# Routing the sample tokens through both row halves of TensorE in the first gather of a mixture-of-experts kernel

## What is computed

```python
h = rmsnorm(x, norm_ffn)                      # x * rsqrt(mean(x*x)) * gain
g_idx = argmax(h @ router_g + b_g)            # one of 4 groups
top_v, top_i = top_k(e_logits[g_idx], 2)      # two of the group's 4 experts
hid = silu(h @ w_gate[e]) * (h @ w_up[e])     # 256 wide
y = sum over the two experts of weight * (hid @ w_down[e])
x = x + y
```

## Time and profile before

| what | value |
|---|---|
| median of 3 runs | 586.61 us (585.15 to 587.17) |
| profiled execution, its own time | 584.05 us |
| its span, first to last instruction | 581.9 us |
| mean granted TensorE clock | 0.995 of full speed |
| PE busy | 558.2 us (96% of the span) |
| DVE, ACT, POOL busy | 247.4, 154.7, 79.4 us |
| moved by transfers | 208.94 MB, mean 359 GB/s |

### The profile page before, as it was taken

The page is one execution under the profiler, slowest core; times in us unless marked ns, Lnnn a source line. Parts: engine busy times, 40 slices in busy tenths (PEclk is TensorE's granted clock), DMA queues, the critical chain, the costliest instruction groups (busy, mean ns, idle before and its releaser), DMA issues. The chain is left out here.

```text
span 581.9 us, 8509 instructions
## 1 busy us (share of the span) xinstructions
PE 558.2 (96%) x3438; PEld 309.4 (53%) x3438; DVE 247.4 (43%) x559; ACT 154.7 (27%) x327; POOL 79.4 (14%) x116
## 2 busy tenths in 40 slices
PE   6999999999999999998999999999999889999993
PEld 5777877544633333337876556667644533333331
DVE  6999783223651112145633415260113642211146
ACT  6132195121301101134235104164003220101023
POOL 5960800000121110000100001000000011220000
PEclk9999999999999999999999999999999999999997
DMA  8995999997999999999999998999699999999872
GB/s 329 415 355 79 222 401 380 375 403 318 363 410 420 419 419 422 395 306 374 390 412 317 409 400 335 304 355 409 256 407 417 381 406 417 420 419 423 358 234 91
DMA packets 40073, 208.94 MB, mean 359 GB/s; under 512 B 12835, under 2 KB 14563, under 8 KB 24192
## 3 DMA queue, kind: packets, MB, share of 16 engines
q1 hardware_dynamic: 30560, 169.93, 74.9%
q0 software_dynamic: 7872, 34.53, 16.6%
q10 hardware_dynamic: 1600, 3.90, 1.7%
HBM read 198.77 MB, written 43.74 MB: 417 GB/s over the span
## 5 line engine op out<-in xcount | busy, mean ns | idle before, releaser
L1513 PE MATMUL bank<-arena 128*64 128x512 f32 x264 | 85.6, 598 | 0.5 <-DVE arena L1853 0.5
L1513 PE MATMUL bank<-ring,arena 128*64 128x512 f32 x232 | 74.7, 598 | 0.1
L2310 PE MATMUL bank<-arena,ring 128*128 128x320 f32 x256 | 71.6, 434 | 0.0
L2310 PEld LDWEIGHTS bank<-arena,ring 128*128 128x128 f32 x256 | 48.0, 190 | 21.4 <-issue 1.6
L1434 PE MATMUL bank<-ring,arena 128*128 128x512 f32 x92 | 40.3, 594 | 1.0 <-PEq L455 0.6
L1513 PEld LDWEIGHTS bank<-arena 128*64 128x64 f32 x264 | 24.0, 136 | 31.5 <-issue 31.3
L1544 PE MATMUL bank<-arena 128*64 128x512 f32 x136 | 39.8, 594 | 0.7 <-ACT arena L1758 0.7
L577 PE MATMUL bank<-xnT,ring 128*128 128x320 f32 x144 | 39.5, 434 | 0.5 <-DVE xnT L896 0.5
L1969 DVE COPY arena<-bank 128x512 f32<-128x512 f32 x14 | 9.7, 692 | 68.3 <-PE bank L1544 68.3
L1544 PE MATMUL bank<-ring,arena 128*64 128x512 f32 x120 | 36.1, 593 | 0.7 <-ACT arena L1758 0.7
L1513 PEld LDWEIGHTS bank<-ring,arena 128*64 128x64 f32 x232 | 20.8, 136 | 24.5 <-issue 24.3
(11 more groups left out here) (446 smaller groups left out, 846.5 us busy)
## 6 DMA issues: line engine op xcount, KB each, us to landing
arena<-in_w_moe SPq DMA_DIRECT2D x50, 1024.0 KB, 17.4
ring<-in_w_moe SPq DMA_DIRECT2D x44, 1024.0 KB, 17.2
arena<-in_stream_b SPq DMA_DIRECT2D x4, 2560.0 KB, 14.8
out_o_d_old<-in_cache_d_g POOLq DMA_DIRECT2D x1, 8448.0 KB, 30.4
arena<-in_stream_a SPq DMA_DIRECT2D x4, 2048.0 KB, 10.8
out_o_d_old<-in_cache_d_g POOLq DMA_DIRECT2D x1, 7680.0 KB, 41.9
out_o_d_old<-in_cache_d_g SPq DMA_DIRECT2D x1, 4608.0 KB, 37.8
ring<-in_w_out_even SPq DMA_DIRECT2D x2, 2048.0 KB, 11.3
```

The lines of the kernel that those rows point to most:

```text
L1513: last = nc.tensor.matmul(c.bank[2 + j % 2][half, :], xgT[:, j % 2, q, half], w[i][q // 4][:, q % 4, :], start=(q == 0), stop=(q == KC - 1))
L2310: last = nc.tensor.matmul(bank(name)[:, 0:TOK], w[:, k, i * P:(i + 1) * P], xnT[:, k, :], start=(k == 0), stop=(k == KC - 1))
```

## The change

It touches `moe_block` alone, in both layers. Tile 2's normed rows and one-hot matrix are laid out on all 128 partitions: partitions 0 to 63 hold columns 0 to 511 of the 64 sample rows, partitions 64 to 127 hold columns 512 to 1023 of the same rows, and `Sf[:, 2]` is there twice. `gather_samples` replaces `gather_first(2)`: the same 8 products, in the order (q, half), where half 0 runs on the rows 0 to 63 of the array into bank 2 and half 1 on the rows 64 to 127 into bank 3. `tmp` for the upper partitions is made by one more DVE instruction on the two columns that `Sf` needs. ACT writes the samples' normed rows with two activations in place of one, and their transfer to `x_rows` runs over 128 partitions with 2 KB each, where it was 64 with 4 KB each. The first copy out of bank 2 is split in two (q = 0, 1 and q = 2, 3), so that there are three `xt_ok` signals for pair 0, and `up(0)` writes bank 4 in place of bank 2.

```diff
@@ -1235,6 +1235,10 @@
     def gathered_rows(j):
 
         return m["xg"][(j - 1) % XG]
+
+    def up_bank(j):
+
+        return 2 + j % 2 if j else 4
 
     def yo_of(j):
 
@@ -1388,7 +1392,7 @@
 
         @block.gpsimd
         def _(pool):
-            nc.gpsimd.memset(xn[64:P, 2], 0.0).then_inc(gather_steps, 1)
+            nc.gpsimd.memset(xn[:, 2], 0.0).then_inc(gather_steps, 1)
 
             def gather(j):
 
@@ -1481,16 +1485,25 @@
             def gather_first(t, first=0, end=KC):
 
                 for q in range(first, end):
-                    last = nc.tensor.matmul(c.bank[2 + q // 4][:, (q % 4) * P:(q % 4 + 1) * P], xn[0:ROWS[t], t, q * P:(q + 1) * P],
-                                            m["Sf"][0:ROWS[t], t].rearrange("p e s -> p (e s)"),
-                                            start=(t == 0 and q % 4 == 0), stop=(t == 2 and q % 4 == 3))
-                    if t == 2 and q % 4 == 3 or t == 0 and q == KC - 1:
+                    last = nc.tensor.matmul(c.bank[2 + q // 4][:, (q % 4) * P:(q % 4 + 1) * P], xn[:, t, q * P:(q + 1) * P],
+                                            m["Sf"][:, t].rearrange("p e s -> p (e s)"), start=(t == 0 and q % 4 == 0), stop=False)
+                    if t == 0 and q == KC - 1:
                         last.then_inc(first_pe, 1)
 
+            def gather_samples():
+
+                for q in range(4):
+                    for h in range(2):
+                        half = slice(64 * h, 64 * h + 64)
+                        last = nc.tensor.matmul(c.bank[2 + h][:, q * P:(q + 1) * P], xn[half, 2, q * P:(q + 1) * P],
+                                                m["Sf"][half, 2].rearrange("p e s -> p (e s)"), start=False, stop=(q == 3))
+                        if q == 3:
+                            last.then_inc(first_pe, 1)
+
             def turn(j):
 
                 gathered(pe, j)
-                pe.wait_ge(xt_ok, 2 * j)
+                pe.wait_ge(xt_ok, 2 * j + 1)
                 for q in range(KC):
                     last = nc.tensor.transpose(c.bank[q // 4][:, (q % 4) * P:(q % 4 + 1) * P], gathered_rows(j)[:, q * P:(q + 1) * P],
                                                c.ident[:, :])
@@ -1502,15 +1515,17 @@
                 if first == 0:
                     piece_arrived(pe, 6 * j)
                     piece_arrived(pe, 6 * j + 1)
-                    pe.wait_ge(xt_ok, 2 * j + 1)
+                    pe.wait_ge(xt_ok, 2 * j + 2 if j else 1)
                 for q in range(first, end):
+                    if j == 0 and q == 2:
+                        pe.wait_ge(xt_ok, 2)
                     if q == KC // 2:
-                        pe.wait_ge(xt_ok, 2 * j + 2)
+                        pe.wait_ge(xt_ok, 2 * j + 3)
                         piece_arrived(pe, 6 * j + 2)
                         piece_arrived(pe, 6 * j + 3)
                     for i in range(2):
                         half = slice(64 * i, 64 * i + 64)
-                        last = nc.tensor.matmul(c.bank[2 + j % 2][half, :], xgT[:, j % 2, q, half], w[i][q // 4][:, q % 4, :],
+                        last = nc.tensor.matmul(c.bank[up_bank(j)][half, :], xgT[:, j % 2, q, half], w[i][q // 4][:, q % 4, :],
                                                 start=(q == 0), stop=(q == KC - 1))
                     if q == KC // 2 - 1:
                         last.then_inc(up_mid, 1)
@@ -1603,8 +1618,8 @@
                 last = nc.tensor.matmul(c.bank[7][:, 64:80], ones, m["sum"][:, u, :], start=(u == 0), stop=(u == 2))
             last.then_inc(pos_pe, 1)
             pe.wait_ge(S0_ok, 2)
-            pe.wait_ge(xn_ok, 3)
-            gather_first(2)
+            pe.wait_ge(xn_ok, 4)
+            gather_samples()
             up(0, 0, 2)
             pe.wait_ge(H_ok, 1)
             pe.wait_ge(S_ok, 1)
@@ -1737,14 +1752,23 @@
             act.dma_start(m["route_in"], x["route_in"][layer]).then_inc(ld, 16)
             for t, rows in enumerate(ROWS):
                 act.wait_ge(added, 2 * t + 2)
-                nc.scalar.activation(xn[0:rows, t], c.resid[0:rows, t], ACT.Square,
+                nc.scalar.activation(xn[:, t] if t < 2 else xgT[0:64, 0].rearrange("p k m -> p (k m)"), c.resid[0:rows, t], ACT.Square,
                                      accum_out=c.stat[0:rows, t:t + 1]).then_inc(sq_ok, 1)
                 act.wait_ge(sq_ok, t + 1)
                 nc.scalar.activation(c.stat[:, 3 + t:4 + t], c.stat[:, t:t + 1], ACT.Sqrt, scale=1.0 / D, bias=c.eps).then_inc(rms_ok, 1)
                 act.wait_ge(rstd_ok, t + 1)
-                nc.scalar.activation(xn[0:rows, t], c.resid[0:rows, t], ACT.Copy, scale=c.stat[0:rows, 6 + t:7 + t]).then_inc(xn_ok, 1)
-                act.wait_ge(xn_ok, t + 1)
-                act.dma_start(x["x_rows"][t * P:t * P + rows, :], xn[0:rows, t]).then_inc(rows_out if t == 2 else first_out, 16)
+                if t < 2:
+                    nc.scalar.activation(xn[:, t], c.resid[:, t], ACT.Copy, scale=c.stat[:, 6 + t:7 + t]).then_inc(xn_ok, 1)
+                    act.wait_ge(xn_ok, t + 1)
+                    act.dma_start(x["x_rows"][t * P:(t + 1) * P, :], xn[:, t]).then_inc(first_out, 16)
+                else:
+                    act.wait_ge(gather_steps, 1)
+                    for h in range(2):
+                        nc.scalar.activation(xn[64 * h:64 * h + 64, 2, 0:512], c.resid[0:64, 2, h * 512:(h + 1) * 512], ACT.Copy,
+                                             scale=c.stat[0:64, 8:9]).then_inc(xn_ok, 1)
+                    act.wait_ge(xn_ok, 4)
+                    act.dma_start(bass.AP(tensor=x["x_rows"].tensor, offset=SEQ * D, ap=[[512, 2], [D, 64], [1, 512]]), xn[:, 2, 0:512])\
+                        .then_inc(rows_out, 16)
             act.wait_ge(earg, 1)
             nc.scalar.activation(m["ge"], m["ge"], ACT.Exp).then_inc(eok, 1)
             act.wait_ge(earg, 2)
@@ -1753,7 +1777,7 @@
                 act.wait_ge(up_pe, j + 1)
                 if j >= 2:
                     act.wait_ge(hid_ok, j - 1)
-                nc.scalar.activation(sg[:, j % 2], c.bank[2 + j % 2][:, 0:FF], ACT.Silu).then_inc(sg_ok, 1)
+                nc.scalar.activation(sg[:, j % 2], c.bank[up_bank(j)][:, 0:FF], ACT.Silu).then_inc(sg_ok, 1)
                 act.wait_ge(ht_pe, j + 1)
                 nc.scalar.copy(hidT[:, j % 2].rearrange("p f m -> p (f m)"), c.bank[6][:, 0:2 * P]).then_inc(ht_ok, 1)
                 act.wait_ge(dn_pe, j + 1)
@@ -1838,11 +1862,11 @@
                 dve.wait_ge(lt_pe, t + 1)
                 v.tensor_copy(m["lgT"][:, t * P:t * P + ROWS[t]], c.bank[5][:, t * P:t * P + ROWS[t]]).then_inc(lt_ok, 1)
 
-            def first_turned(h):
-
-                dve.wait_ge(first_pe, h + 2)
-                v.tensor_tensor(xgT[:, 0, 4 * h:4 * h + 4, :], c.bank[2 + h][:, :].rearrange("p (k r) -> p k r", k=4),
-                                c.gains[:, gain, 4 * h:4 * h + 4].unsqueeze(2).broadcast_to([P, 4, P]), ALU.mult).then_inc(xt_ok, 1)
+            def first_turned(k0, k1):
+
+                dve.wait_ge(first_pe, 2 + k0 // 4)
+                v.tensor_tensor(xgT[:, 0, k0:k1, :], c.bank[2 + k0 // 4][:, k0 % 4 * P:(k0 % 4 + k1 - k0) * P].rearrange("p (k r) -> p k r", r=P),
+                                c.gains[:, gain, k0:k1].unsqueeze(2).broadcast_to([P, k1 - k0, P]), ALU.mult).then_inc(xt_ok, 1)
 
             def xg_turned(j):
 
@@ -1864,6 +1888,7 @@
             dve.wait_ge(ld, ROUTER_LOADS)
             v.tensor_copy(m["tri"], k[:, P:3 * P]).then_inc(tri_ok, 1)
             v.memset(m["z"], 0.0)
+            v.memset(m["tmp"][64:P, 2], 0.0)
             v.memset(m["rank"], 0.0)
             v.memset(m["sel"][:, :, 2, :], 0.0)
             link(v.memset(m["sum"][:, 2, :], 0.0))
@@ -1903,8 +1928,11 @@
             def place(a, b):
 
                 dve.wait_ge(pos_pe, 1 + a // 2)
-                v.scalar_tensor_tensor(m["tmp"][:, a:b], c.bank[7][:, 16 * a:16 * b].rearrange("p (t e) -> p t e", e=E_N), 1.0,
-                                       m["sum"][:, a:b], ALU.add, ALU.mult).then_inc(tmp_ok, 1)
+                if a == 2:
+                    v.scalar_tensor_tensor(m["tmp"][64:P, 2, 0:2], c.bank[7][0:64, 32:34], 1.0, m["sum"][0:64, 2, 0:2], ALU.add, ALU.mult)
+                rows = P if a == 0 else 64
+                v.scalar_tensor_tensor(m["tmp"][0:rows, a:b], c.bank[7][0:rows, 16 * a:16 * b].rearrange("p (t e) -> p t e", e=E_N), 1.0,
+                                       m["sum"][0:rows, a:b], ALU.add, ALU.mult).then_inc(tmp_ok, 1)
                 dve.wait_ge(tmp_ok, 1 + a // 2)
                 v.tensor_tensor(m["Sf"][:, a:b], iota[:, 1:CAP + 1].unsqueeze(1).unsqueeze(1).broadcast_to([P, b - a, 2, CAP]),
                                 m["tmp"][:, a:b, 0:2].unsqueeze(3).broadcast_to([P, b - a, 2, CAP]), ALU.is_equal).then_inc(S0_ok, 1)
@@ -1929,8 +1957,9 @@
             v.tensor_scalar(m["far"], pk, float(CAP), float(SKIP), ALU.is_ge, ALU.mult)
```

(7 more changed lines are left out.)

## The result

The changed kernel takes 607.1 us (median of 5 runs, 606.57 to 607.68) against 586.92 us for the kernel before on the same chip: ratio 1.0352, 95% interval 1.0326 to 1.0379. It is slower by 20 us. The forecast was 586.8, with a chance of 0.89 for no change; its range ended at 588.0, and the slower rival stood at 588.4 with a chance of 0.08.

A forecast was written before the change was run, and what follows sets the result against it. PE was taken to bound the kernel, busy 96% of the span. Layer 0's +0.45 us and layer 1's -0.26 gave together +0.2 on the median of 586.61, so 586.8 us; range 585.4 to 588.0.

The forecast's parts named there:

- the slower rival: Samples' rows take 9.2 us to land; layer 0 loses 2.0 us, layer 1 gains 0.26: 588.4 us, chance 0.08.
- the samples' transfer: Samples' normed rows to x_rows: 7.6 us to landing instead of 6.5, making layer 0's gather(1) and turn(1) 0.45 us late.
- if each DMA engine takes a row of ours: Samples' transfer: an engine alternates our row with a q1 packet, so 8 rows cost 2.9 us instead of 1.8.
- The upper bound: Samples' transfer: at most 9.2 us to landing, taken from the slowest transfer of 128 rows of 4 KB.
- lateness costs nothing: Layer 1: the samples' transfer coming 0.45 us later costs nothing, because turn(1) stands behind down(0).
- The row halves: Samples' gather on PE: 16 instructions on two row halves take 1.16 us instead of 2.05.
- DVE's first copy: Copy out of bank 2, now 256 columns wide: starts at 463.47 in layer 1, as before to 0.02 us.
- the twelve matmuls: Small matmuls on PE after up(0, 0, 2): DVE's L, which they wait for, stays hidden by 0.05 us.
- The rival without overlap: The two row halves of the samples' gather don't overlap; up(0) starts 0.5 us later per layer: 587.6 us, chance 0.05.
- the second small DVE instruction: In place, between the count of places and Sf: adds 0.08 us to the path, at most 0.17.
- the gain of 0.26: up(0, 0, 2) starts 0.26 us earlier, bounds 0.17 and 0.34; arrives in layer 1, swallowed in layer 0.
- ACT's two activations: Writing the samples' normed rows: end over 2 us ahead of Sf, with the transfer's issue 0.05 us later.

The follow-up runs named there:

- late_sp_wait: Changed kernel with SP's wait for POOL's small memset behind gather(1) moved from the first pair to the fourth: 621.01 us, ratio 1.0585.
- outer_2: Kernel before, with the destination of the samples' 64 rows of 4 KB written as 2 x 32 rows: 605.78 us, ratio 1.0337.
- outer_8: Kernel before, with the destination of the samples' 64 rows of 4 KB written as 8 x 8 rows: 590.15 us, ratio 1.0045.
- old_transfer: Changed kernel with the samples' rows sent as before, 64 rows of 4 KB, and a third activation filling the upper partitions: 588.43 us, ratio 1.0034.
- rows_2kb: Kernel before, with the samples' rows sent as two transfers of 64 rows of 2 KB, left and right half: 587.47 us, ratio 1.0019.
- before_busy: Kernel before, plus one unread matmul of 384 columns ahead of PE's wait for the samples' one-hot matrix: 586.23 us, ratio 0.9995.
- two_transfers: Changed kernel with the samples' rows sent by two transfers of 64 rows of 2 KB instead of one: 590.45 us, ratio 1.0072.
- split_only: Kernel before, with the split first copy and up(0) in bank 4 but without the row halves: 587.02 us, ratio 1.0005.
- outer_4: Kernel before, with the destination of the samples' 64 rows of 4 KB written as 4 x 16 rows: 598.34 us, ratio 1.0199.

## Why the prediction was wrong

**The term that failed** is the one I had called the only one whose price the trace doesn't show: the samples' transfer. I worked out 7.6 us to landing, with 9.2 as the upper bound; it took 15.93. The step that failed in it is "if each DMA engine takes a row of ours": I divided the 128 rows by 16 engines. The price of a row was about right: as two transfers over all 16 engines it landed 8.1 us after the first issue (0.6 us between the two issues and 7.5 for the second). In late_sp_wait, with the weights loading beside it, the 64 rows of an engine spread over 21.65 us in layer 0, 0.34 a row, where I had put 0.28 + 0.08 = 0.36. The spacing of 0.46 us in outer_2 is likewise the 0.44 of the prediction, one row of ours and one packet of q1 in turn; the rule of the Trainium skill that the prediction quoted, a whole packet of 9 to 17 descriptors at a time, is not what these records show, and they decide here. It is the number of engines that was 2. The upper bound was no bound, since every row of the trace that I took it from had 64 or 128 as its outermost dimension; I never asked what in the new access pattern had no such row. The Trainium skill, DMA: Bandwidth & Descriptors, section Why a DMA increments its semaphore by 16 and not by 1, states it: the number of engines is the largest up to 16 that divides the slowest dimension of both access patterns, each of them writing one closing increment. The trace agrees: 66, 68, 72 and 130 packets for 2, 4, 8 and 2. I had drawn on another section of that page and missed this one.

**The mechanism** of the slower rival was right, the transfer ahead of `gather(1)`, and that ahead of `turn(1)` in layer 0; its size, 9.2 us to landing, was not. For layer 1 I wrote that lateness costs nothing, since `turn(1)` stands behind `down(0)`. That holds for 0.45 us (outer_8's first gather in layer 1 comes 1.7 us later than before and PE waits for no rows there) and not for 8: layer 1's transfer cost 9.8 us. I had listed SP's wait behind `gather(1)` among what orders the work, and never priced what it holds back.

**What held.** The row halves took 1.16 us, as line 645 did. DVE's first copy started 1.26 us after the gather (155.78 - 154.52), 1.20 forecast; `up(0)` 1.83 after it, 1.76 forecast; the twelve matmuls 3.70, 3.63 forecast, with `L` hidden behind `up(0, 0, 2)`. The rival without overlap is out.

**What was mis-sized** beside it: the second small DVE instruction cost 0.17 (153.89 - 153.72), not 0.08, and in layer 0 `Sf` took 0.37 instead of 0.31. From the first instruction of `place` to the twelve matmuls it is 4.50 us there (158.22 - 153.72); before it was 4.54 (line 1906 at 152.12, the twelve at 156.66). In layer 1 it was 4.53 before (461.63 to 466.16) and, in old_transfer, whose clock stayed up there, 4.41 (464.26 to 468.67). So the gain of 0.26 was 0.04 in layer 0 and 0.12 in layer 1. ACT's two activations took 1.47 us where one took 1.15, and the transfer's issue came 0.3 later, not 0.05.

**What stays open:** the 4.1 us that the changed kernel with two transfers still loses. Named are 0.7 us of more waiting for gathered rows in layer 0 (0.91 against 0.20) and, in the profiled execution, 1.6 at the low clock in layer 1 and the waits and the lower clock at the end of layer 0 shown above, where PE had waited 1.21 us in the kernel before. That last part is not the change's alone, for the profiles of rows_2kb and before_busy, within 0.2% of the kernel before, have 2.20 and 2.12 us of waiting for ACT there and the lower clock behind it. How much goes with the clock can be estimated from the mean granted clock of each execution: the kernel before took 587.8 us on average in the seven of its 18 executions beside two_transfers with a clock up to 0.990, and 584.8 in the eight from 0.994 on; two_transfers took 590.6 in the six of its seven up to 0.990. So at a like clock some 2.8 of the 4.1 us remain, and their cause is open.

## What to carry to other kernels

When a transfer's access pattern is rewritten, count its outermost dimension on both sides: bytes and rows unchanged, 64 rows cost 0.45%, 2% and 3.4% of this kernel on 8, 4 and 2 engines. In all transfers here the number of packets on the queue, less the rows, told on how many engines they ran, at one look. And a bound taken from rows of the trace bounds only what those rows have in common with the new operation.

## What was not expected of the hardware

- A transfer on 2 engines is slowed by the weights' loads far more than its own bytes say: 17.1 us to the first gather with SP held back, 27.0 with the loads beside it.
- The issue on ACT's queue lasted 1.03 to 1.18 us for the three-dimensional destinations, on 2, 4 or 8 engines alike, and 0.51 for 64 rows.
- After 9 us without work PE ran at the lower of its two levels (1.2 GHz) for about 6 us; but the fall in layer 1's first `up` came in some executions only, in the profiles of the changed kernel, two_transfers, split_only, outer_4 and outer_8, and not in the other nine.
